# A chunked delta-rule scan on one core: a turn moved to another PSUM bank, a new order on four engines, and fewer waits

## The reference, cut to what matters

```
def step(s, inp):
    r_t, w_t, k_t, v_t, aa_t, bb_t = inp
    sa = einsum('bhij,bhj->bhi', s, aa_t)
    s = s * w_t[:, :, None, :] + sa[..., None] * bb_t[:, :, None, :] + v_t[..., None] * k_t[:, :, None, :]
    return s, einsum('bhij,bhj->bhi', s, r_t)
s_last, ys = scan(step, s0, (r, w, k, v, -kk, kk * a))
y = group norm of ys over each head, + (sum of r * k * r_k over the head) * v, times the gate g
```

## Time and profile before

| | us |
|---|---|
| median of 3 runs | 3327.82 |
| lowest, highest | 3323.55, 3328.18 |
| profiled execution, its own time | 3325.93 |
| span of its trace | 3324.1 |
| PE busy | 3063.9 |
| DVE busy | 1648.2 |
| ACT busy | 1157.4 |
| POOL busy | 927.6 |

### The profile page before, as it was taken

How to read it: one execution, slowest core, us unless ns; L and a number is a source line. 1 busy time by engine, 2 the same in 40 slices (tenths; PEclk the granted TensorE clock), 3 DMA queues, 4 the chain that set the end, 5 groups by cost and what they waited for, 6 DMA issues and landing times.

```text
span 3324.1 us, 73605 instructions
## 1 busy us (share of the span) xinstructions
PE 3063.9 (92%) x32244; PEld 2963.6 (89%) x32244; DVE 1648.2 (50%) x1702; ACT 1157.4 (35%) x1339; POOL 927.6 (28%) x505
## 2 busy tenths in 40 slices
PE   6999799999999998699968888887989999999997
PEld 5889799999999998699967777776989999999997
DVE  5555564544444456102206777774354545444445
ACT  4633332221222224433325666665132222212222
POOL 1222122222222223223313344434112222222221
PEclk9999899999999999799988999998989999999998
DMA  2111011111111110332222222212111111111111
GB/s 100 43 42 34 32 39 45 45 45 45 44 41 44 45 45 26 122 138 85 92 92 59 69 61 59 69 45 84 46 33 45 45 45 45 43 47 40 44 45 67
DMA packets 87562, 186.10 MB, mean 56 GB/s; under 512 B 28896, under 2 KB 51936, under 8 KB 87264
## 3 DMA queue, kind: packets, MB, share of 16 engines
q1 hardware_dynamic: 80352, 154.73, 14.7%
q10 hardware_dynamic: 6912, 26.84, 2.0%
HBM read 145.01 MB, written 36.53 MB: 55 GB/s over the span
## 4 chain that ended last, share of the span: by engine, by line
PE 82%; DVE 9%; ACT 4%; POOL 2%; issue 2%; DMA 1%; SPq 0%; ACTq 0%; DVEq 0%; POOLq 0%
PE PS L1113 67%; PE PS L1301 10%; PE PS L1141 2%; ACT T L471 2%; DVE T L1566 1%; DVE G L1566 1%; POOL HL L913 1%; DVE X L1566 1%; DVE M L1581 1%; POOL WL L913 1%; DVE HF L1576 1%; PE PS L1254 1%; DVE NN L1566 1%; ACT L471 1%; DVE T L1576 1%
## 5 line engine op out<-in xcount | busy, mean ns | idle before, releaser
L913 POOL TENSOR_TENSOR WL<-RAW,WH 128x1024 fp32r<-128x1024 f32 x204 | 498.4, 2443 | 1583.9 <-ACT WH L471 1579.9
L1113 PE MATMUL PS<-HH,WH 128*128 128x364 f32 x3312 | 738.2, 331 | 39.2 <-POOL WL L913 13.5
L1113 PE MATMUL PS<-HH,WL 128*128 128x364 f32 x3312 | 737.9, 331 | 0.0
L1113 PE MATMUL PS<-HL,WH 128*128 128x364 f32 x3312 | 734.2, 330 | 0.0
L1113 PEld LDWEIGHTS PS<-HH,WH 128*128 128x128 f32 x3312 | 577.9, 189 | 45.7 <-POOL WL L913 22.5
L1113 PEld LDWEIGHTS PS<-HH,WL 128*128 128x128 f32 x3312 | 582.5, 190 | 0.0
L1113 PEld LDWEIGHTS PS<-HL,WH 128*128 128x128 f32 x3312 | 579.1, 189 | 0.0
L1566 DVE TENSOR_TENSOR X<-PS,X 128x1092 f32<-128x1092 f32 x224 | 290.2, 1295 | 281.0 <-PE PS L1113 276.3
L1576 DVE SCALAR_TENSOR_TENSOR T<-T,FP 128x1092 f32<-128x1092 f32 x192 | 414.0, 2156 | 6.8
L471 ACT ACTIVATE WH<-RAW 128x1024 fp32r<-128x1024 f32 x204 | 216.5, 1061 | 369.1 <-PE PS L1113 346.1
L471 ACT ACTIVATE T<-PS 128x1092 f32<-128x1092 f32 (+1 forms) x125 | 135.4, 1083 | 595.6 <-PE PS L1113 559.9
(11 more groups left out here) (164 smaller groups left out, 3593.4 us busy)
## 6 DMA issues: line engine op xcount, KB each, us to landing
RAW<-weights SPq DMA_DIRECT2D x204, 512.0 KB, 3.6
scratch<-T ACTq DMA_DIRECT2D x32, 546.0 KB, 2.9
scratch<-SR ACTq DMA_DIRECT2D x16, 546.0 KB, 2.9
X<-xT SPq DMA_DIRECT2D x8, 546.0 KB, 7.9
yT<-HF SPq DMA_DIRECT2D x8, 546.0 KB, 2.9
T<-scratch_m SPq DMA_DIRECT2D x8, 512.0 KB, 4.1
LW<-scratch SPq DMA_DIRECT2D x16, 192.0 KB, 2.5
KK<-scratch SPq DMA_DIRECT2D x16, 192.0 KB, 3.2
```

The costliest lines, as they stand in the source:

```text
L913: pool.tensor_tensor(out, full, hi, ALU.subtract).then_inc(*t.made(event))
L1113: mm = pe.matmul(acc[:, j, :], a, b[:, j * CW:(j + 1) * CW], start=(i == 0 and q == 0), stop=(i == len(blocks) - 1 and q == 2))
```

## The change

It has four parts, all in the scan.

- `value_turn` is gone. Its matmuls write bank 7 instead of bank 3 and stand between the matmuls of the last level's `grow(5)`, pair by pair, in a new function `values_and_last` at the end of the interval. ScalarE's `values` reads bank 7 and moves from behind `group_ln` to the place ahead of `turned(5)`. `seed`, which overwrites bank 7, waits for `k_vt`.
- The lists of TensorE, VectorE, ScalarE and GpSimd are put into another order.
- The helpers get an argument `own`, which is False everywhere in the scan: no instruction there waits for its engine's last instruction. Where one reads what the engine itself wrote just before, a wait for that very result is written out (`key_square`, `norm_exp`, `growth`, `group_exp`, `taken_key`, `grown_taken`, `gated`, `weighted`).
- SyncE's loads also wait for `k_tv` of the interval before.

```diff
                     if job >= -1:
                         sp.wait_ge(*t.at("k_g", 8 * (job + 2)))
                         sp.wait_ge(*t.at("k_bonus", job + 2))
+                        sp.wait_ge(*t.at("k_tv", 2 * (job + 2)))
...
-            def run(out, in_, func, event, bias=0.0, scale=1.0, n=None):
-                if t.latest:
+            def run(out, in_, func, event, bias=0.0, scale=1.0, n=None, own=True):
+                if own and t.latest:
                     act.wait_ge(*t.own())
...
                     if has_k:
-                        run(X2[:, klo:khi], X2[:, klo:khi], ACT.Exp, "k_rn", scale=-0.5, bias=0.5 * LNS * float(np.log(2.0)))
+                        act.wait_ge(*t.at("k_ln", job + 4))
+                        run(X2[:, klo:khi], X2[:, klo:khi], ACT.Exp, "k_rn", scale=-0.5, bias=0.5 * LNS * float(np.log(2.0)), own=False)
...
                         for h in range(HEADS):
-                            run(UV[HALF[1 - h], pa:pz, h, :], bank(3, pz - pa, HALF[1 - h]), ACT.Copy, "k_vt")
+                            run(UV[HALF[1 - h], pa:pz, h, :], bank(7, pz - pa, HALF[1 - h]), ACT.Copy, "k_vt", own=False)
...
+                unit_key()
                 unit_plus()
-                unit_key()
                 receptance()
-                grown_key()
                 taken_key()
                 grown_taken()
+                grown_key()
...
-                    held(("k_bx", inv + 1), ("k_nti", inv + 1), ("k_mc", mc * inv), ("k_mtc", (LEVELS - 1) * inv))
+                    held(("k_bx", inv + 1), ("k_nti", inv + 1), ("k_vt", 2 * inv + 2), ("k_mtc", (LEVELS - 1) * inv))
...
+                def values_and_last():
+
+                    if has_l:
+                        held(("k_bm", lm * inv + lm), ("k_mtc", (LEVELS - 1) * inv + lm), ("k_mc", mc * inv + mc))
+                    for i in range(6):
+                        if has_p and pa + i < pz:
+                            for h in range(HEADS):
+                                mul(tile(7, 1 - h, i), VV[HALF[h], (pa + i) * CHUNK:(pa + i + 1) * CHUNK], IST[HALF[h], :],
+                                    "k_tv" if pa + i == pz - 1 else None)
+                        if has_l and la + i < lz:
+                            for h in range(HEADS):
+                                mul(tile(5, 1 - h, i), B[HALF[1 - h], i, :], MT[HALF[1 - h], la + i, :],
+                                    "k_mb" if la + i == lz - 1 else None, False)
```

More of the change, by code:

```diff
@@ L757, in turned @@
                         act.wait_ge(*t.at("k_mb", MB_ALL * inv + (4 * k if k < LEVELS - 1 else MB_ALL)))
-                        run(MT[:, la:lz, :], bank(5, lz - la), ACT.Copy, "k_mtc")
+                        run(MT[:, la:lz, :], bank(5, lz - la), ACT.Copy, "k_mtc", own=False)
                 def scaled_key():
@@ L792, in solved_values @@
                         for h in range(HEADS):
-                            run(UV[HALF[h], a:z, h, :], bank(4, z - a, HALF[h]), ACT.Copy, "k_sae")
+                            run(UV[HALF[h], a:z, h, :], bank(4, z - a, HALF[h]), ACT.Copy, "k_sae", own=False)
                 def solved_keys():
@@ L798, in solved_keys @@
                         act.wait_ge(*t.at("k_w", 2 * job + 2))
-                        run(W[:, 0:z - a, :], bank(3, z - a), ACT.Copy, "k_we")
+                        run(W[:, 0:z - a, :], bank(3, z - a), ACT.Copy, "k_we", own=False)
                 def decay_in():
@@ L820, in centred_square @@
                         act.wait_ge(*t.next("k_cent"))
-                        run(q1, flat(Y)[:, na * CHUNK:nz * CHUNK], ACT.Square, "k_csq")
+                        run(q1, flat(Y)[:, na * CHUNK:nz * CHUNK], ACT.Square, "k_csq", own=False)
                 def affine():
@@ L827, in affine @@
                         act.wait_ge(*t.next("k_pn"))
-                        run(y, y, ACT.Identity, "k_pt", scale=PQ[:, nf, 0:1], bias=PQ[:, nf, 1:2])
+                        run(y, y, ACT.Identity, "k_pt", scale=PQ[:, nf, 0:1], bias=PQ[:, nf, 1:2], own=False)
                 def values():
@@ L858, in outputs_y @@
                         act.wait_ge(*t.next("k_y", 2))
-                        run(Y[:, a:z, :], bank(1, z - a), ACT.Copy, "k_ys")
+                        run(Y[:, a:z, :], bank(1, z - a), ACT.Copy, "k_ys", own=False)
+                spread_out()
+                centred_square()
+                decay_in()
+                solved_keys()
+                growth()
+                solved_values()
+                turned(1)
+                scaled_key()
                 key_factor()
-                spread_out()
-                scaled_key()
-                solved_keys()
-                solved_values()
+                group_ln()
+                turned(2)
+                group_exp()
                 key_square()
-                decay_in()
-                centred_square()
-                growth()
-                turned(1)
-                group_ln()
-                values()
-                turned(2)
+                affine()
+                turned(3)
                 norm_ln()
-                group_exp()
-                norm_exp()
-                turned(3)
-                affine()
                 keys()
                 turned(4)
+                norm_exp()
                 outputs_y()
+                values()
                 turned(5)
@@ L1007, in _, with tt @@
             assert n == W_OUT
-            def tt(out, x, y, op, event):
-                if t.latest:
+            def tt(out, x, y, op, event, own=True):
+                if own and t.latest:
                     pool.wait_ge(*t.own())
@@ L1477, in products @@
                                     AR[HALF[h], i, :, :].rearrange("p s c -> p (s c)"), "k_g" if i == gz - 1 else None)
-                def value_turn():
-                    if not has_p:
-                        return
-                    held(("k_rt", job + 1) if has_s else ("k_nm", inv + 1))
-                    for i in range(pa, pz):
-                        for h in range(HEADS):
-                            mul(tile(3, 1 - h, i - pa), VV[HALF[h], i * CHUNK:(i + 1) * CHUNK], IST[HALF[h], :],
-                                "k_tv" if i == pz - 1 else None)
                 def key_turn():
@@ L1887, in bonus @@
                             dve.wait_ge(*t.next("k_padd"))
[L1888 removed]
+                        tt(BON[:, lo:hi], PS[:, 2, 0:hi - lo], VV[:, lo:hi], ALU.mult, "k_bonus", own=False)
                 def masked(g):
```

133 lines of the change are left out of this document (68 added, 65 removed).

## The result

The changed kernel took 3338.47 us (median of 7 runs, 3333.96 to 3342.57), the kernel before on the same chip 3325.49 us (7 runs, 3322.60 to 3328.58). The ratio is 1.0036, 95% interval 1.0023 to 1.0049: slower by 8 to 16 us. The forecast was faster, 3312 us. It was wrong in its direction, and the measured time lies 0.5 us above the range of 3293 to 3338 us.

The account below looks back on a forecast made before the run. No engine was taken as full in the scan; TensorE waits in short round trips. 0.9 us less per period, times 23, is 20.7 us; a quarter given back leaves -15: 3311, or 3312 from the median, range 3293 to 3338.

Parts of the forecast that it names:

- No engine is full there: In the scan, TensorE waits in short pieces, as each inverse level is a round trip with copying engines; period 22.1 us.
- issue: Trace row of TensorE waits in the scan that nothing shown ends, read as waiting for its instructions: 0.9 us per interval.
- the walk: One scan interval's sections laid out by durations and inputs: 21.1 us in the old order, 20.2 us in the new.
- I give back a quarter.: A quarter of the scan's 20.7 us gain is lost as faster TensorE meets its instruction fetch sooner, leaving -15 us.
- The 0.70 are gone: Values beside the last level on other quarters save TensorE 0.70 us of issue per interval, 17.5 to 16.8 us.
- The step: From one ready VectorE or ScalarE instruction to the next in the scan, without own wait: -0.08 us, bounds +0.04 and -0.16.
- the fixed 0.16 us: Size-independent part of VectorE's instruction B in the scan, which the next instruction might cover; half was taken.
- The rival without overlap: VectorE and ScalarE steps in the scan stay +0.04 us, the period grows by 0.4 us: 3337 us; chance 0.17.
- a rival at 0.09: ScalarE becomes the scan's bound: two more table loads push `keys` behind `lower(0)`, period 0.4 us longer, 3337 us; chance 0.09.
- These are zero: SyncE's scan loads come about 1.5 us later but are used an interval later, so they were priced at zero.
- the fetch takes it back: TensorE's instruction records stream no faster beside the scan's loads; issue grows to 1.7 us, time within 3 us of 3326; chance 0.14.

Follow-up runs that it names:

- tiny loads: Scan loads cut to 4 columns from the second head pair on (stale data), in the kernel before: 3324.67 us, and in the changed kernel: 3326.99 us.

## Why the prediction was wrong

- **The period's bound.** "No engine is full there: TensorE waits in short pieces", each a round trip. Half right. "issue" was read correctly as TensorE waiting for its instructions (all 34 pieces in before end 2.3 to 3.0 us behind the start of a block), but put down as a term of 0.9 us that stays. It is better read as what remains visible of a second pace. An interval takes 128/23 = 5.57 blocks; at the 3.8 us between them that before shows where the loads take under a tenth of the DMA engines, these are 21.2 us, more than the 20.2 that the walk gave. This is an estimate and partly circular, since the distance was measured in a kernel whose period is 22.1 us, and part of it is TensorE's own pace: the shortest distance in before is 3.4 us, which would make 19 us for an interval. That the blocks forbid 20.2 us is not shown.
- **"I give back a quarter."** This is the step that failed. The forecast let "issue" grow from 0.9 to 1.0 to 1.3 us; it went to 2.6. In the old order, with own waits alone removed, it already doubled (19.7 to 40.2 us). The walk's 0.9 us of gain were given back in full, which tiny loads do not change (47.6 us of "issue", a period of 22.0 us), and 0.6 us on top through the loads. (By its own reason, 0.9 of 4.5 us, the share was a fifth and not a quarter, which makes 1 us of the sum.)
- **The value matmuls.** "The 0.70 are gone": they lie beside the last level as foretold (IST,VV and MT,B start 0.01 to 0.02 us apart). But a matmul hidden on another quarter was not free: leaving out 784 of these instructions gained 15 us, with three blocks less.
- **The step.** Forecast -0.08 us, measured -0.08 to -0.09 on VectorE and -0.09 to -0.11 on ScalarE (median -0.083 and -0.101 over the steps below zero from 1760 to 2260 us). Right. With a foreign and an own wait it is +0.10, with the own wait alone +0.04, and +0.11 with the own waits put back. To take half of the fixed 0.16 us was the author's choice between two bounds; no run shows what the fixed part consists of. The rival without overlap gave the right time (3337) for a wrong reason, and by luck: its waits are said to add up to 4.7 us, but the terms given make 5.1 us, or about 3346 us.
- **ScalarE's table loads.** Priced at nothing, against a rival at 0.09. Right, shown by their removal. There were 85, 92 were forecast.
- **SyncE's loads.** "About 1.5 us later ... These are zero." Wrong: later loads alone cost 6.6 us in before, and without the loads' bytes after is level with before. Against NN they start 2.3 us later, from 1.6 us ahead of it to 0.7 behind. The forecast asked who reads the data, and not what else the DMA engines carry at that moment.
- **The rival "the fetch takes it back"** had the mechanism (in after 4.6 us from block to block beside the loads, 3.8 without) and 14%. It named an issue of 1.7 us and a time within 3 us of before. It names the loads, but prices nothing for them beyond that, and their cost carries the time to the other side.

## What to carry to other kernels

Where TensorE runs streams of small matmuls and a trace shows short waits that nothing ends, look whether the pauses end at a fixed distance behind the instruction blocks (here 2.3 to 3.0 us, all 34 of before). If they do, fewer instructions can gain where better cover gains little (here 15 us for 784 of them in after, some 5, with overlapping intervals, in the old order). Then a matmul "hidden" on a free quarter can have a price (those 15 us), and a load's place matters by what else the DMA engines carry at that moment, not only by who reads it (6.6 us here). Ask of each wait removed whether the fetch was hidden under it.

## What was not expected of the hardware

- The same scan of 128x384 took 1726 ns in before and 948 ns in after, with the same shapes. The traces show what differs. In before GpSimd's `NI<-NN,IST` starts 0.02 to 0.03 us ahead of `scan` in all 22 intervals from 1760 to 2260 us, and `scan` lasts 0.7 to 0.85 us longer than where nothing runs beside it or it starts first; that operation takes 0.87 to 1.00 us. In before without own waits `scan` starts first, 0.16 us ahead in all 22, and takes 0.81 to 0.95 us; now the GpSimd operation takes 1.4 to 1.6 us. In after 14 of 22 scans have no GpSimd operation beside them; where `NI<-NN,IST` starts 0.60 us ahead (7 scans of 128x320), `scan` takes 1.08 us and not 0.81. First before, then before without own waits:

```profile
1795.04 0.87 POOL L1012 TENSOR_TENSOR NI<-NN,IST 128x320 f32<-128x320 f32 x1 [11.45 <-DVE NN L1566]
1795.06 1.66 DVE L1861 TENSOR_TENSOR_SCAN Z<-SCAN,LW 128x384 f32<-128x384 f32 x1
```

```profile
1792.91 0.95 DVE L1880 TENSOR_TENSOR_SCAN Z<-SCAN,LW 128x384 f32<-128x384 f32 x1
1793.08 1.44 POOL L1016 TENSOR_TENSOR NI<-NN,IST 128x320 f32<-128x320 f32 x1 [12.43 <-DVE NN L1587]
```

In these 44 pairs the one that starts second is the long one: `scan` with 1.66 to 1.80 us, `NI<-NN,IST` with 1.4 to 1.6 us. What makes it long is not shown. `key` (1105 and 548 ns) was not looked at in this way. From 1760 to 2260 us VectorE is busy for 363.2 us in before and 316.1 without own waits; the kernel's time falls by 6 us only.
- The instruction queue q8 moves packets of 16,384 bytes, and their number follows TensorE's instructions: 254 in before and in after, 251 with 784 less, 258 with 859 more, 261 with 1,718 more. It is one for each 254 matmuls and weight loads. TensorE resumes from most of its long pauses 2.2 to 3.1 us after a block's packet begins (29 of 33; 1980.98 to 1983.21 in the one shown), and two blocks lay 5.8 us apart beside a burst of loads at 60% of the DMA engines.
- A satisfied second wait at every tenth matmul costs 43 ns of time each, at every fifth 33 ns. Why these are not the same is open.
- An instruction of VectorE or ScalarE whose inputs are ready starts before its predecessor's end where no own wait stands (in after 0.08 to 0.09 us on VectorE, 0.09 to 0.11 on ScalarE), and behind it with one (in before 0.04 to 0.11 us on VectorE, 0.03 or 0.09 on ScalarE).
